# Seven half products instead of eight for the gate and up matrices of layer 1's feed-forward block

## The reference

```python
FFN_DIM = 2816
def swiglu(h, wg, wu, wd):
    return (jax.nn.silu(h @ wg) * (h @ wu)) @ wd
```

## Time and profile before

| | us |
|---|---|
| time, median of 3 runs (lowest, highest) | 2483.44 (2482.28, 2484.17) |
| span of the profiled execution, first to last instruction | 2480.8 |
| median time less that span | 2.6 |
| PE busy | 2402.4 (97%) |
| DVE, ACT, POOL busy | 941.1, 887.4, 852.9 |
| feed-forward block of layer 1, first unit to first unit of the next stage (1432.6 to about 1798.1 in the span) | 365.5 |

### The profile page before, as it was taken

The page is one execution under the profiler, slowest core; times in us unless marked ns, Lnnn a source line. Parts: engine busy times, 40 slices in busy tenths (PEclk is TensorE's granted clock), DMA queues, the critical chain, the costliest instruction groups (busy, mean ns, idle before and its releaser), DMA issues.

```text
span 2480.8 us, 34754 instructions
## 1 busy us (share of the span) xinstructions
PE 2402.4 (97%) x13237; PEld 1892.2 (76%) x13237; DVE 941.1 (38%) x1440; ACT 887.4 (36%) x1690; POOL 852.9 (34%) x705
## 2 busy tenths in 40 slices
PE   6999999999999999899899999999999998999998
PEld 4776666788888888687577778888887656888887
DVE  5556632411111113555357331111527666422322
ACT  4336632321121122343556332222423564422331
POOL 1223002223323233352002345445644532444443
PEclk9999999999999999999899999999999999999999
DMA  8630027322222213421020243333333201333332
GB/s 268 187 111 10 2 90 239 89 67 60 62 65 59 68 53 108 122 68 37 7 44 18 86 120 100 93 101 94 103 93 79 80 1 35 94 102 94 98 98 76
DMA packets 336116, 209.76 MB, mean 85 GB/s; under 512 B 29315, under 2 KB 308588, under 8 KB 335986
## 3 DMA queue, kind: packets, MB, share of 16 engines
q1 hardware_dynamic: 333330, 201.98, 28.1%
q10 hardware_dynamic: 2592, 5.96, 0.7%
q0 software_dynamic: 64, 0.04, 0.0%
HBM read 205.82 MB, written 2.12 MB: 84 GB/s over the span
## 4 chain that ended last, share of the span: by engine, by line
PE 86%; DVE 4%; issue 4%; ACT 2%; DMA 1%; POOL 1%; SPq 0%; DVEq 0%; ACTq 0%; POOLq 0%
PE G L1670 22%; PE G L1671 21%; PE G L1672 21%; PE G L1889 5%; PE G L1917 4%; PE G L1902 4%; PE G L1754 1%; POOL wlo L961 1%; PE G L1861 1%; PE G L1935 1%; PE G L1694 1%; PE G L1712 1%; PE G L1695 1%; PE G L1696 1%; DVE ssq L2189 1%
## 5 line engine op out<-in xcount | busy, mean ns | idle before, releaser
L961 POOL TENSOR_TENSOR wlo<-raw,whi 128x512 fp32r<-128x512 f32 x564 | 745.9, 1344 | 1386.6 <-ACT whi L1155 1386.5
L1155 ACT ACTIVATE whi<-raw 128x512 fp32r<-128x512 f32 x564 | 325.4, 624 | 1199.8 <-PE G L1672 1081.4
L1670 PE MATMUL G<-big_a,whi 128*128 128x512 f32 x2016 | 740.3, 367 | 2.2 <-POOL wlo L961 1.5
L1671 PE MATMUL G<-big_a,wlo 128*128 128x512 f32 x2016 | 728.1, 361 | 0.0
L1672 PE MATMUL G<-big_a,whi 128*128 128x512 f32 x2016 | 724.5, 359 | 0.0
L1670 PEld LDWEIGHTS G<-big_a,whi 128*128 128x128 f32 x2016 | 379.9, 188 | 76.3 <-issue 12.6
L1671 PEld LDWEIGHTS G<-big_a,wlo 128*128 128x128 f32 x2016 | 379.8, 188 | 63.3 <-issue 6.7
L1672 PEld LDWEIGHTS G<-big_a,whi 128*128 128x128 f32 x2016 | 378.8, 188 | 60.2
L1670 PE MATMUL G<-big_b,whi 128*128 128x512 f32 x856 | 315.3, 368 | 0.9 <-issue 0.9
L1671 PE MATMUL G<-big_b,wlo 128*128 128x512 f32 x856 | 315.5, 369 | 0.0
L1672 PE MATMUL G<-big_b,whi 128*128 128x512 f32 x856 | 314.3, 367 | 0.0
(11 more groups left out here) (270 smaller groups left out, 2215.2 us busy)
## 6 DMA issues: line engine op xcount, KB each, us to landing
raw<-in_l_ada_w_dram SPq DMA_DIRECT2D x84, 512.0 KB, 4.8
raw<-in_l_ffn_w_gate_dram SPq DMA_DIRECT2D x44, 512.0 KB, 3.8
raw<-in_l_ffn_w_up_dram SPq DMA_DIRECT2D x44, 512.0 KB, 3.8
raw<-in_l_ffn_w_down_dram SPq DMA_DIRECT2D x32, 512.0 KB, 4.0
raw<-in_w_up_dram SPq DMA_DIRECT2D x32, 512.0 KB, 4.0
raw<-in_w_down_dram SPq DMA_DIRECT2D x32, 512.0 KB, 4.0
raw<-in_w_in_dram SPq DMA_DIRECT2D x28, 512.0 KB, 3.8
raw<-in_l_w_in_dram SPq DMA_DIRECT2D x24, 512.0 KB, 4.0
```

Of the source, the lines that this page charges most:

```text
L961: ins = pool.tensor_tensor(wlo[:, u % 2, k:k + 4], raw[:, r % RING, k:k + 4], whi[:, u % 2, k:k + 4].bitcast(F32), ALU.subtract)
L1155: act.activation(whi[:, u % 2, k:k + 4], raw[:, r % RING, k:k + 4], ACT.Copy).then_inc(hi_done, 1)
L1670: pe.matmul(o, whi[:, u % 2, k], rlo[:, k, t0:t0 + w], start=k == order[0], stop=False)
L1671: pe.matmul(o, wlo[:, u % 2, k], rhi[:, k, t0:t0 + w], start=False, stop=False)
```

## The change

The gate and up matrices of all tiles but the first two are no longer multiplied unit by unit. Two neighbouring tiles of one matrix form a **set**: a block of 256 output channels x 1024 input channels x 512 tokens. It is cut in two in each direction: the weights into a11, a12, a21, a22 (even and odd input tiles; first and second output tile), the tokens into two halves of 256. A set is then made of seven products of half size by Winograd's form of Strassen's scheme, each 4 input tiles x 3 matmuls = 12 matmuls of 256 columns, 84 in a set in place of 48 of 512 columns. There are 20 sets in three sections (6, 8, 6); the first two tiles stay four plain units.

What each engine does for it:

- DVE makes the weight sums W1, W2, a11-a21 (in place) and W4 of each set, four instructions of 128x512 out of and into SBUF, one set ahead (`fast_sum`). It also puts the seven products together: three additions of 128x512 and one of 128x256 with one operand in PSUM, in up sets two multiplications of 128x512 in SBUF, and for each hidden tile a remainder `alo` in SBUF.
- ACT rounds the seven weight operands (7 x 128x512 in place of 4), each into a half slot of `whi`, four half slots ahead of PE; copies the first product (128x256) out of PSUM; takes Silu of a whole gate set (128x1024); rounds each hidden tile.
- POOL makes all seven remainders of a set (7 x 128x512 in place of 4), 14 for a gate and up pair.
- `norm(3)` gets one more ACT instruction per channel tile, a full-precision copy of h in `rows_b` (`full`), and DVE's next `tmp` waits for it. Behind it `fast_operands` makes the four sums of activations for both halves: eight DVE sums, eight ACT roundings, eight DVE remainders, each 128x512.
- The loops over units become written-out code; the loads are the same blocks of 512 KB, in the order gate, gate, up, up.

```diff
+            def fast_lowers(sec):                                        # POOL
+                for st in sec["sets"]:
+                    p = st["p"]
+                    a11, a12, a21, a22 = blocks(st)
+                    for q, src in ((0, a11), (1, a12), (2, W2), (3, W1), (4, a21), (5, W4), (6, a22)):
+                        s = slot_of(sec, 7 * p + q)
+                        pool.wait_ge(PH["fast", "hi"], 7 * p + q + 1)
+                        ins = pool.tensor_tensor(half_slot(wlo, s), src, half_slot(whi, s).bitcast(F32), ALU.subtract)
+                        if q >= 5:
+                            ins.then_inc(raw_free[st["r"][q - 5] % RING], 1)
+                        else:
+                            ins.then_inc(PH["fast", "lop"], 1)
...
+            def fast_upper(sec, i):                                      # ACT
+                if q == 0:
+                    act.wait_ge(landed[r % RING], ring_total[r])
+                elif 2 <= q <= 5:
+                    act.wait_ge(PH["fast", "sum"], 4 * p + (2, 1, 3, 4)[q - 2])
+                act.activation(half_slot(whi, slot_of(sec, i)), (a11, a12, W2, W1, a21, W4, a22)[q],
+                               ACT.Copy).then_inc(PH["fast", "hi"], 1)
...
+                    for q in range(7):                                   # ACT, fast_section
+                        act.wait_ge(done, 7 * p + q + 1)
+                        if q == 0:
+                            act.activation(s1, b1, ACT.Copy).then_inc(PH["fast", "copy"], 1)
+                        fast_next(sec, 7 * p + q + 4)
+                        if st["kind"] == "up" and q == 0:
+                            act.wait_ge(out, 4 * (p - 1) + 4)
+                            act.activation(sg, sg, ACT.Silu).then_inc(PH["fast", "silu"], 1)
+                        if st["kind"] == "gate" and at and q < 2:
+                            hidden_tiles(sec["sets"][at - 1], q)
...
+            def fast_operands(i):                                        # ACT, ahead of upper(u0 + 2)
+                for half in range(2):
+                    for at, a in enumerate(T_ORDER):
+                        act.wait_ge(PH["fast", "tsum"], 4 * half + at + 1)
+                        act.activation(t_pieces(a, half)[0], t_sum(a, half), ACT.Copy).then_inc(PH["fast", "thi"], 1)
...
             norm(3, X_ONLY, lambda k, q: mod[:, 1, 24 + k, q:q + 1], ("up", 1, 0, 1))      # ACT
-            ffn(1, FFN_CHUNKS, X_ONLY, 4)
+            fast_operands(3)
+            fast_ffn(1, FFN_CHUNKS, X_ONLY, 4)
...
+                    for q in range(7):                                   # PE, fast_section
+                        if q >= 5:
+                            pe.wait_ge(raw_free[r % RING], r // RING + 1)
+                        else:
+                            pe.wait_ge(PH["fast", "lop"], 5 * p + q + 1)
...
+                        for j in range(4):
+                            xhi, xlo = operands(q, j)
+                            pe.matmul(outs[q], half_slot(whi, s)[:, j], xlo, start=j == 0, stop=False)
+                            pe.matmul(outs[q], half_slot(wlo, s)[:, j], xhi, start=False, stop=False)
+                            mm = pe.matmul(outs[q], half_slot(whi, s)[:, j], xhi, start=False, stop=j == 3)
+                        mm.then_inc(done, 1)
...
+                    for q in range(7):                                   # DVE, fast_section
+                        if q == 2:
+                            dve.wait_ge(done, 7 * p + 3)
+                            dve.tensor_tensor(c[:, 0:2], b26, twice(s1), ALU.add).then_inc(out, 1)
+                        elif q == 4:
+                            dve.wait_ge(done, 7 * p + 5)
+                            dve.tensor_tensor(mid, b57, twice(c[:, 1]), ALU.add).then_inc(out, 1)
+                            dve.tensor_tensor(c[:, 3], b57[:, 1], mid[:, 0], ALU.add).then_inc(out, 1)
+                            if up:
+                                dve.tensor_tensor(c[:, 0::3], c[:, 0::3], sg[:, 0::3], ALU.mult).then_inc(mult, 1)
+                        elif q == 6:
+                            dve.wait_ge(done, 7 * p + 7)
+                            dve.tensor_tensor(c[:, 1:3], b34, mid, ALU.add).then_inc(out, 1)
+                            if up:
+                                dve.tensor_tensor(c[:, 1:3], c[:, 1:3], sg[:, 1:3], ALU.mult).then_inc(mult, 1)
+                        if ahead:
+                            if q in (2, 3):
+                                fast_sum(ahead, q - 2)
+                            elif q == 5:
+                                fast_sum(ahead, 2)
+                            elif q == 6:
+                                fast_sum(ahead, 3)
+                        if not up and at and q < 2:
+                            hidden_tile(sec["sets"][at - 1], q)
```

More of the change, by code:

```diff
@@ L284, in build, with wslot @@
         plan = {}
-        cnt = {"r": 0, "u": 0, "g": 0, "a": 0}
+        cnt = {"r": 0, "u": 0, "g": 0, "a": 0, "p": 0, "pair": 0, "w4": None}
+        flips = []
+        def wslot(u):
+            return (u + sum(1 for first in flips if u >= first)) % 2
         ring_dmas = []
@@ L884, in square_matrix, with fast_ffn @@
                         load(r0 + b, [(w[:, :, bass.ds((j * 4 + b) * P, P)], P)], j)
+            def fast_ffn(l, ups, down, chunks):
+                for c, (f0, nf) in enumerate(chunks):
+                    if c == 0:
+                        for b in range(4):
+                            m = P * (f0 + b // 2)
+                            load(plan["up", l, c, b][1], [(ups[b % 2][:, :, m:m + P], P)])
+                            if b < 2:
+                                ada(*HOSTED[1 + 2 * l][b])
+                    for st in plan["sec", l, c]["sets"]:
+                        for i, r in enumerate(st["r"]):
+                            m = P * (f0 + st["tile"] + i)
+                            load(r, [(ups[0 if st["kind"] == "gate" else 1][:, :, m:m + P], P)])
+                    r0 = plan["down", l, c, 0][1]
+                    with sp.Fori(0, 2) as j:
+                        for b in range(4):
+                            load(r0 + b, [(down[:, f0:f0 + nf, bass.ds((j * 4 + b) * P, P)], P)], j, rows=nf)
             def ffn(l, ups, down, chunks):
@@ new lines, in fast_ffn @@
+            def fast_ffn(l, chunks, ranges, h_ready):
+                for c, (f0, nf) in enumerate(chunks):
+                    if c == 0:
+                        first_units([("up", l, 0, 0), ("up", l, 0, 1)], lambda b: ranges, h_ready)
+                        ada_turn(*HOSTED[1 + 2 * l][1])
+                        for b in range(2, 4):
+                            unit(("up", l, 0, b), hhi, hlo, ranges)
+                    sec = plan["sec", l, c]
+                    fast_section(sec)
+                    p = sec["sets"][-1]["p"]
+                    pe.wait_ge(PH["fast", "copy"], p + 1)
+                    for b in range(KD):
+                        if 0 < b < 4:
+                            pe.wait_ge(PH["fast", "out"], 4 * p + (1, 3, 4)[b - 1])
+                        unit(("down", l, c, b), ahi, alo, ranges, k_tiles=nf,
+                             h_ready=(f"ffn{l}", "lo", f0) if b == 0 else None)
@@ L2212, in norm @@
                             dve.wait_ge(*when((f"norm{i}", "h"), k - 1))
+                        if k >= 2 and i == 3:
+                            dve.wait_ge(PH["fast", "full"], k - 1)
                         for q, (t0, w) in enumerate(ranges):
```

295 lines of the change are left out of this document (279 added, 16 removed).

## The result

The changed kernel takes 2500.56 us (median of 4 runs, 2498.48 to 2504.43) against 2482.86 us of the kernel before in the same measurement (4 runs, 2481.56 to 2484.17): ratio 1.0071, 95% interval 1.0057 to 1.0086. It is slower. The profiled span is 2496.3 us, 15.5 more than before; it belongs to the shortest of the four runs. Forecast were 2502 us and a span of 2499.8.

A forecast was written before the change was run, and what follows sets the result against it. PE's matmuls bound the kernel before; POOL would bound the sections. Stall 8.7, clock 2.3, sections 5.5, last sets 1.0 and ends 1.5 sum to +19.0 us, about 2502 us; range 2489 to 2519.

The forecast's parts named there:

- PE's side: In the sections: matmuls of 256 columns 0.122 us apart, a set 10.2 us; 12.3 us won if PE stayed the bound.
- POOL's side: In the sections: 1.25 us a remainder, 0.47 more per colliding DVE instruction; POOL becomes the bound, 5.5 us more.
- The size of the port's price: In the sections: POOL loses 0.47 us per collision, not DVE's whole 0.68 us; the whole-instruction rival gave 2523, chance 0.05.
- ACT and DVE keep up: In a set of 11.6 us: ACT needs about 6.2 us, DVE fits; W4 is tightest, about 0.5 us left after rounding.
- PSUM and loads: In the sections: no wait of PE for PSUM halves, and no load on the path.
- The opening: Ahead of the third unit: DVE's sums behind ada_columns delay ACT's rounding; PE stalls 8.7 us (7.7 to 10.5).
- The clock: Behind the opening stall: half speed for 4.6 us, costing 2.3 us (0 to 3.5).
- Ends: At the ends of sections: the first down unit waits for the last hidden tiles, 1.5 us in all (0 to 4).
- the fourth rival: In the sections: PE stays the bound because DVE's instructions find POOL idle; 12.3 us given back, 2484; chance 0.10.

The follow-up runs named there:

- e2: Changed kernel, but weight sums of 17 sets read PSUM (times zero) in place of one SBUF operand, giving wrong values; 2481.51 us.
- e4 to e6: Changed kernel with DVE making a11's remainder in 17 sets ahead of W2 (2508.58 us); with e1's edit, behind W2 (2495.71); likewise, gate sets alone (2497.09).
- e1: Changed kernel, but DVE makes the sums of activations ahead of the late ada_columns instead of behind it; 2494.34 us.
- e7: Changed kernel, but ACT rounds the weights of the third and fourth unit ahead of fast_operands, DVE's order kept; 2501.38 us.
- e8: Changed kernel with the edits of e1 and e2 together (wrong values as in e2); 2471.30 us, ratio 0.9950 to the kernel before.
- e11: Changed kernel with e1's edit; ACT copies a22, a11 and a12 into idle PSUM banks for DVE's sums, a12 into the third product's; 2476.99 us.

## Why the prediction was right

The mechanism came as described: POOL became the bound of the sections through its turns with DVE, and DVE's order made the stall. The nearness of the number (2500.56 for 2502) is in part luck: the stall was 0.5 us shorter than forecast, the sections cost 0.3 us less and the ends 1.2 us more, and the medians moved by 17.7 us where the block grew by 19.4.

- **PE's side.** 0.122 us a matmul was forecast; it was 0.120 (product 1.44 us, set 10.08). The 0.2264 us at 512 columns was a little low as well: a unit takes 5.44 us, and the 40 units took 217.6 us and not 217.3. Both readings divided a stretch by a count that takes in the matmuls at its edges. The 3 us too much for the new products had no effect, since PE was not the bound.
- **POOL's side.** Right: 1.25 us a remainder and 0.45 more with a turn of DVE behind it, 100 such turns, pairs in 23.0 us, POOL without idle time, 223.8 us for the sections as summed. e2 showed that it is the port and not POOL's instructions alone: without 68 collisions the sections took 21 us less and met PE's floor of 202.8. POOL's mean fell by 0.22 and 0.30 us an instruction there (1594 to 1371 ns, and 1680 to 1376 for those out of scratch); over 138 instructions, 35 us for 68 collisions, or 0.5 each.
- **The size of the port's price.** The Trainium skill, "SBUF — State Buffer", section "SBUF: two separate sides", holds the port for the whole instruction. In kind it agrees again; POOL loses 0.45 us and not 0.68 in the rows above.
- **ACT and DVE keep up.** Right, and by as little as forecast: in every second set POOL starts on W4 0.39 us after ACT has rounded it, where 0.5 was forecast. W2 is as tight, 0.40 us, which the prediction did not name. e4 to e6 showed that the margin did not take a seventh instruction.
- **PSUM and loads.** No wait of PE for either inside a section.
- **The opening.** The chain was as described; 0.5 us shorter, since the sums follow at 0.61 us with POOL idle and not at 0.66. e1 removed 7.0 of 8.2 us and e7 moved the stall, which shows DVE's order as the cause.
- **The clock.** Half speed from 1451.58 to about 1456.5, 4.9 us, where the earlier trace rows had 4.6.
- **Ends.** 1.2 us too low, within its bounds. No run separates the parts of this term beyond the wait of 1.55 us.
- **A slip in the chances.** What is left of the fourth rival's 0.10 beside the 0.02 is 0.08 and not 0.07.
- **What I missed** lay in my expectations for experiments: that e4 to e6 would pay, that e1 would leave nothing behind, and twice that freeing the port would create no wait elsewhere.

## What to carry to other kernels

Count, for a change that trades PE time for vector work, the instructions of DVE with both operands in SBUF that run while POOL is busy: each costs POOL about half a microsecond here, and 68 of them alone turned a gain of 12 us (e8) into a loss of 11 (e1). An operand in an idle PSUM bank removes the collision, but the bank must be one that PE asks for late. And look at what a new block of work in an in-order program stands behind and in front of: here one call's place cost 8 us, with a drop of the clock among them.

## What the runs showed that I had not expected

- ACT's copy of 128x512 from SBUF into PSUM takes 0.59 us (49 of them), and three more of them in a set cost next to nothing: sections of 203.2 us against 202.8 without them (e8).
- DVE's sum with an operand in PSUM takes 0.68 us while POOL works, in both forms (685 ns with PSUM times zero, e2; L2921 in the changed kernel), where the weight sums out of SBUF took 0.68 to 1.78 us, depending on where POOL stood.
- Matmuls of 256 columns, each with its own weight load, follow each other at 0.120 us with no long one between, whole sets of 84 in a row (e2).
- Spans of kernels that are the same outside one block differ there, by up to 3.8 us from the mark in the next stage to the end (679.9 in e11, 683.7 in e7), more than a change of 0.1% is worth; distances inside one trace are steadier.
